# Moving the weight ring from 96 to 64 bytes past a multiple of 128, with all large tiles at multiples of 128

## The reference

```
h = rmsnorm(x, g_mix);  z = h @ w_in                      # 36 column tiles of 128
a = silu(layernorm(causal_conv31(a_val * sigmoid(a_gt)))) @ w_a_out
s = (sc_b * causal_conv3(sc_c * sc_v)) @ w_b_out
x = x + (g_a * a + g_b * s) @ w_o
u = rmsnorm(x, g_ffn) @ w_up                              # 2 x 2816 columns
x = x + (gelu(causal_conv3(u_gate)) * u_value) @ w_down
x = x + sigmoid(rmsnorm(x, g_ple) @ w_ple_gate) * (p @ w_ple);  x = rmsnorm(x, g_final)
# second block
y = concat(window attention with sinks, differential attention)(rmsnorm(x) @ w_in_2)
x = x + rmsnorm(y @ w_out_2)
x = x + rmsnorm((gelu(c_gate) * c_value) @ w_down_2),  c = causal_conv3(rmsnorm(x) @ w_up_2)   # 2 x 4096 columns
```

## The kernel before, in words

| tile | role | before | after |
|---|---|---|---|
| raw, w_hi, w_lo (ring), column 0 | stationary; moving in units 1 to 3 of `down2` | 96 | 64 |
| ring from unit 4 of `down2` on | moving | 128 | 128 |
| h_hi, h_lo, h2_hi, h2_lo, X, f_hi, f_lo | moving (f stationary in `down2`) | 128 | 128 |
| s_hi/lo, a_hi/lo, p_hi/lo | moving | 192 | 0 |
| y_hi, y_lo | moving | 64 | 128 |
| src, tmp, sq, scales, ev, cg, cv | VectorE's and ScalarE's own | 128 | 128 |

## Time and profile before

### The profile page before, as it was taken

One profiled execution on the slowest core, in us unless ns is written; L12 is line 12 of the kernel. 1 busy time (PEld: TensorE's weight loads), 2 busy tenths in 40 slices (PEclk: granted clock), 3 DMA queues, 4 the chain that ended last, 5 costly groups with the idle time before them and its releaser, 6 DMA issues. The chain is left out here.

```text
span 807.8 us, 16945 instructions
## 1 busy us (share of the span) xinstructions
PE 766.2 (95%) x5954; PEld 737.2 (91%) x5954; DVE 602.2 (75%) x1058; ACT 449.6 (56%) x756; POOL 264.2 (33%) x160
## 2 busy tenths in 40 slices
PE   6889899899999999999899999789999999999996
PEld 5879899899999999999889998789999999988885
DVE  6899976867888888434957686489999999973333
ACT  7444344656665655445655565677666666654431
POOL 0356644464222212345654011641122211222220
PEclk9999999999999999999999999989999999999999
DMA  8445453455555567544433332524555555666551
GB/s 282 147 144 195 150 191 129 157 177 190 182 185 195 188 204 245 187 151 153 144 123 123 105 105 80 180 80 164 192 191 183 184 186 192 217 195 196 186 180 52
DMA packets 37771, 135.44 MB, mean 168 GB/s; under 512 B 4448, under 2 KB 4704, under 8 KB 37728
## 3 DMA queue, kind: packets, MB, share of 16 engines
q1 hardware_dynamic: 37728, 134.86, 50.3%
HBM read 133.80 MB, written 1.05 MB: 167 GB/s over the span
## 5 line engine op out<-in xcount | busy, mean ns | idle before, releaser
L1638 PE MATMUL bank<-h_hi,w_hi 128*128 128x256 f32 x1424 | 406.3, 285 | 22.4 <-DVE h_lo L1056 13.1
L1639 PE MATMUL bank<-h_lo,w_hi 128*128 128x256 f32 x1424 | 401.5, 282 | 0.0
L1640 PE MATMUL bank<-h_hi,w_lo 128*128 128x256 f32 x1424 | 401.2, 282 | 0.0
L545 POOL TENSOR_TENSOR w_lo<-raw,w_hi 128x1024 fp32r<-128x1024 f32 (+2 forms) x78 | 192.9, 2476 | 395.9 <-ACT w_hi L703 395.8
L703 ACT ACTIVATE w_hi<-raw 128x1024 fp32r<-128x1024 f32 (+2 forms) x246 | 261.9, 1067 | 85.4 <-PE bank L1971 41.6
L1638 PEld LDWEIGHTS bank<-h_hi,w_hi 128*128 128x128 f32 x1424 | 272.1, 191 | 29.6 <-issue 20.7
L1044 DVE TENSOR_TENSOR w_lo<-raw,w_hi 128x1024 fp32r<-128x1024 f32 (+1 forms) x168 | 216.4, 1290 | 108.7 <-ACT w_hi L703 108.6
L1639 PEld LDWEIGHTS bank<-h_lo,w_hi 128*128 128x128 f32 x1424 | 272.2, 191 | 0.0
L1640 PEld LDWEIGHTS bank<-h_hi,w_lo 128*128 128x128 f32 x1424 | 271.9, 191 | 0.0
L1084 DVE TENSOR_TENSOR bank<-bank,scales 128x256 f32<-128x256 f32 x124 | 52.9, 430 | 27.7 <-PE bank L1640 13.8
L1311 DVE TENSOR_TENSOR f_lo<-src,f_hi 128x256 f32 (+1 forms) x54 | 60.7, 1124 | 0.5 <-ACT f_hi L850 0.5
(11 more groups left out here) (198 smaller groups left out, 928.1 us busy)
## 6 DMA issues: line engine op xcount, KB each, us to landing
raw<-in_w_up SPq DMA_DIRECT2D x108, 512.0 KB, 3.3
raw<-in_w_in SPq DMA_DIRECT2D x54, 512.0 KB, 3.4
raw<-in_w_down SPq DMA_DIRECT2D x32, 512.0 KB, 3.8
raw<-in_w_down SPq DMA_DIRECT2D x16, 704.0 KB, 4.1
raw<-in_w_o SPq DMA_DIRECT2D x8, 512.0 KB, 3.3
raw<-in_w_gate SPq DMA_DIRECT2D x8, 512.0 KB, 3.4
raw<-in_w_out SPq DMA_DIRECT2D x8, 512.0 KB, 3.3
raw<-in_w_b_out SPq DMA_DIRECT2D x4, 512.0 KB, 3.4
```

Source lines behind the costliest of these rows:

```text
L545: nc.gpsimd.tensor_tensor(w_lo[s][:, cols], raw[s][:, cols], w_hi[s][:, cols].bitcast(f32), ALU.subtract).then_inc(lo_ready[s], 1)
L1638: nc.tensor.matmul(ps, wh, hi[:, k, :], start=start and n == 0, stop=False)
L1639: nc.tensor.matmul(ps, wh, lo[:, k, :], start=False, stop=False)
L1640: last = nc.tensor.matmul(ps, wl, hi[:, k, :], start=False, stop=stop and n == len(ks) - 1)
```

## The change

`RING_PAST` becomes 64, the alignment of tiles of 1024 bytes and more becomes 128, and the two small tiles `o_ms` and `o_rstd` share one. No instruction is added, removed or reordered; operands start at other bytes, as in the table above. `first_col` follows `RING_PAST`, so that from unit 4 of `down2` on the data begins at column 16 instead of 8.

```
-RING_PAST = 32
+RING_PAST = 64
...
         def aligned(offset, size):
-            step = 64 if size >= 1024 else 32
+            step = 128 if size >= 1024 else 32
             return (offset + step - 1) // step * step
...
         o_ss = sb("o_ss", [P, 2, 2])
-        o_ms, o_rstd = sb("o_ms", [P, 2]), sb("o_rstd", [P, 2])
+        o_small = sb("o_small", [P, 4])
+        o_ms, o_rstd = o_small[:, 0:2], o_small[:, 2:4]
```

## The result

| | before | after |
|---|---|---|
| median, 20 runs of each, same chip | 809.28 us (807.03 to 811.19) | 811.20 us (808.7 to 813.56) |
| ratio after / before | | 1.0022, 95% interval 1.0013 to 1.0031 |
| profiled execution, its span | 809.72, 807.8 us | 812.44, 810.5 us |

The change costs 0.2%, inside the 0.3% that I called no change. I forecast 792; the range of 778 to 820 holds the result, the direction does not.

The account below looks back on a forecast made before the run. TensorE's matmul spacing was taken as the bound. Terms 15.7 + 1.6 + 0.5 + 0.7 + 0.2 - 0.7 - 1.0 = 17.0 us off 808.5 gave 791.5, stated as 792, with a range of 778 to 820.

Parts of the forecast that it names:

- What bounds the kernel: Whole kernel: TensorE, busy for 95% of the span; the end is set by how often it starts a matmul.
- the count of 4700: h and f products: 4800 matmuls less at most 120 at half clock, counted as 4700, each gaining 3.33 ns.
- the main term: h and f products, weights moving from 96 to 64: 116.7 to 113.3 ns a matmul, 15.7 us saved.
- s, a, p: 240 matmuls of the s, a and p products: 120.0 to 113.3 ns, 1.6 us saved.
- y: 192 y products: 118.2 to 113.3 ns, 0.9 us, of which half was counted, 0.5 in the sum.
- `o` and the first units: Stretches at 118 instead of 116.7 ns, some 24 units of 24 matmuls: 0.7 us more saved.
- Units 1 to 3 of `down2`: Moving operand goes from 96 to 64: 36 matmuls gain 6.7 ns each, 0.2 us saved.
- the ring's other users: ScalarE's rounding and VectorE's rest: ten nanoseconds cost nothing under cover; on VectorE in `up2` 0.03 us a turn.
- VectorE's cap: `up2`: VectorE works 10.82 us a loop turn, capping better cases; at 113.3 ns a turn takes 10.88, so it holds.
- The one that ended slower: Rival: relative place decides, 64 bytes apart is worse than 32; 118.3 or 120 ns, 816 to 824 us; chance 0.33.
- No change: Rival: weights' place does not matter, or 64 is as good as 32; 807 to 808.5 us; chance 0.18.
- The whole loss: Rival: full-clock loss goes entirely or nearly, bound 106.7 ns, 39 us at most; 770 to 785 us; chance 0.10.

Follow-up runs that it names:

- experiment 1: Changed kernel with the ring at 64 past a multiple of 128, other large tiles in steps of 64, h and f at distance 0: 820.1 us, ratio 1.0154.
- experiment 3: Kernel of experiment 2 with only the ring moved, to 128 (distance 0 for h): 820.6 us, ratio to before 1.0147.
- experiment 4: Kernel of experiment 2 with the ring moved to 32 (distance 96 for h), two more small tiles sharing one: 820.3 us, ratio to before 1.0142.
- experiment 2: Changed kernel with the ring left at 96, other large tiles at multiples of 128: 809.0 us, ratio to before 1.0003.
- experiment 6: The changed kernel again, nothing edited, for a second profile: 811.68 us, one run.
- experiment 9: The kernel of experiment 5 again, unedited: 805.4 us, ratio to before 0.9943.
- 7a: Changed kernel with three extra small matmuls between units in every loop turn of `up` and `up2`: 820.54 us, one run.
- experiment 5: Kernel of experiment 2 with the ring moved to 192 (distance 192 for h), small tiles packed into one: 806.3 us, ratio to before 0.9950.

## Why the prediction was wrong

**What bounds the kernel** held. TensorE's spacing sets the end, and experiments 1, 3 and 4 confirm it from the other side: with 3.3 ns more a matmul (4700 of them, 15.5 us) the spans grew by 10.2 to 11.3 us (818.0, 819.1 and 818.6 against 807.8). The missing 4 to 5 us show what the count of 4700 had wrong. From the first product of a stage to the first of the next, `up`, `down` and `up2` took 9.1, 9.6 and 9.1 us longer, and `in2` 0.8 each time. But `gate` took 24.3 or 24.4 us in all twelve profiles, with mean spacings from 114.0 to 119.9 ns, and `in` took 118.6, 119.5 and 119.8 us against 119.1 before, where its 864 products alone would give 2.5 more. These 1056 of the 4700 products do not set the end: pauses between them take up what the spacing gives or costs.

**The step that failed is the main term**, 4700 matmuls from 116.7 to 113.3 ns, 15.7 us. I took the 113.3 from `down2`, "both operands at multiples of 64", 16/17 of the column rate. The reason was wrong: with both operands at multiples of 64 and 0 apart, the main loop gets 120.0 (experiments 1 and 3). The value exists at distance 64, but as one of two. In the profile after, the h and f products got it only in 15 units of `in` and some short stretches of `in2`; the long loops had 117.8, and by the spacing the term came out as +2.5 us (+3.4, `gate` +0.1, `in` -0.9), of the other sign. I had called the choice weak for the missing row; what I did not consider is that one pair could have two steady spacings. The trace of before did show a hint that I booked as unit borders: `o`, with `up2`'s places, at 118.2 against 116.7. From the starts, 179 products of `o` without a pause ran at 117.8 there, and at 116.7 in experiment 2, at the same places: distance 32 has two spacings as well.

**The small terms.** s, a, p: predicted 1.6 us, got 1.3 by the spacing, but only 0.7 in the time of the three stages; `a_out` went from 360 to 340 ns a group as said. Right value, and again for a wrong reason, since those pairs are 192 apart. y: predicted 0.5, got 0.4 by the mean spacing, nothing visible in the row. `o` and the first units: predicted 0.7, `o` got 19.1 / 54 / 3 = 117.9, nothing. Units 1 to 3 of `down2`, predicted 226.7 ns with the moving operand at 64, stayed at 9 matmuls in 2.11 us, 234 ns (after, in order of time):

```profile
716.38 0.40 PE L1970 MATMUL bank<-w_hi,f_hi 128*128 128x512 f32 x1
...
718.49 0.40 PE L1970 MATMUL bank<-w_hi,f_hi 128*128 128x512 f32 x1
```

The rest of `down2`, the ring's other users and VectorE's cap came out as worked.

**The rivals.** The one that ended slower was right that the relative place decides and that the kernel gets slower, and its price was too high: it took 118.3 ns or more, for +7.8 us or more, where the long loops got 117.8 and the spans +2.7. Its rule, that 64 lies between 32 and 96, fails too, since 64 also has 113.3. "No change" had the result, with neither of its reasons: the ring's place matters, by up to 11.6 us between experiments 2 and 3, and 64 is as good as 32 only as a sum of better and worse stretches. The whole loss never went: 113.3 ns is the lowest that any full-clock stretch of 256 columns settled in. My two checks "a_out must equal `up2` unless the distance matters" and "340, 350, 355 or 360" were of use: 340 in `a_out`, 353.5 in `up2`, a number that no case had.

**What stays open.** What picks the spacing at a break. It is partly chance, as experiments 6 and 9 show, and it is not even: at distance 64 the long loops came out at 117.8 in all three profiles with these places (after, 6, 7a), and the fastest of the 20 timed runs, 808.7, leaves no room for an `up2` at 113.3 (about 804, an estimate: 811.2 less 1536 x 4.45 ns); at distance 192 both came up. Why the distance acts at all, and whether 256 is its period, was not tried.

## What to carry to other kernels

When TensorE sets the end, compare the spacing of its starts with the column rate, for each pair of start bytes; in this kernel the difference of moving and stationary start, mod 256, was worth 113.3 to 120.0 ns for the same instruction; 0 and 96 are to be avoided, they cost 1.4 to 1.5% of the kernel. A row of one shape or one pair does not price another, and one pair can have two steady values: look at several stretches, and profile the same kernel twice, before a spacing goes into a sum. The best place found, distance 192, gives 0.5 to 0.6% (two timings), and its runs cover 11.5 us where those of the kernel before cover 5.6.

## What I had not expected

- A steady spacing that differs between stretches of one execution with the same operands, 113.3 and 117.8 ns, and that holds from the break to the next one, for 1439 matmuls in `up2`.
- Two executions of one program with the long stretches the other way round: `up` 117.8 and 113.3, `up2` 113.3 and 117.8 (experiments 5 and 9).
- The ring's place alone moves the spacing from 116.7 to 120.0 ns (experiments 2 and 3), with every other tile in place. That the whole change moved the time by only 0.2% hides this.
